# A hybrid convolution and retention layer on eight cores: weight sums on one engine, two products joined in PSUM, interleaved norm chains

## The reference

```
hcat = x @ w_in                                   # B, C, h | q, k, v, g, 512 columns each
y_conv = B * causal_conv3(C * h)
o = chunkwise retention of rotary(q), rotary(k), v (4 heads, chunks of 128)
y_ret = silu(g) * head_group_norm(o)
x = layer_norm(ALPHA * x + concat(y_conv, y_ret) @ w_out)
ff = square(relu(x @ w_ff1)) @ w_ff2              # 1024 -> 4096 -> 1024
ple = sigmoid(x @ w_ple_gate) * (p @ w_ple_proj)
x = layer_norm(ALPHA * x + ff + ple)
```

## Time and profile before

| | us |
|---|---|
| median of 6 runs | 880.86 |
| lowest, highest | 879.99, 882.60 |
| the profiled execution's own time | 880.31 |
| its span on the slowest core (core 4) | 878.8 |
| PE busy in it | 777.3 (88%) |
| DVE, POOL, ACT busy | 565.4, 299.5, 267.5 |

### The profile page before, as it was taken

The page is one execution under the profiler, slowest core; times in us unless marked ns, Lnnn a source line. Parts: engine busy times, 40 slices in busy tenths (PEclk is TensorE's granted clock), DMA queues, the critical chain, the costliest instruction groups (busy, mean ns, idle before and its releaser), DMA issues.

```text
span 878.8 us, 12280 instructions; the slowest of 8 cores (875.8 to 878.8 us)
## 1 busy us (share of the span) xinstructions
PE 777.3 (88%) x3884; PEld 363.4 (41%) x3960; DVE 565.4 (64%) x767; ACT 267.5 (30%) x499; POOL 299.5 (34%) x252
## 2 busy tenths in 40 slices
PE   4999999998998869878999999769999999999920
PEld 1444455554454324323444444324444444444400
DVE  4556745566655725555478999715764477999991
ACT  2222246646662154335332000113343322000021
POOL 9000046555653613341000125403661000124574
PEclk9999999999999989999999999899999999999965
DMA  9995215310029664546821540586679920441012
GB/s 125 162 194 104 59 38 89 57 46 28 26 74 256 103 131 99 141 121 132 144 49 28 94 83 13 106 158 120 178 170 229 164 51 12 85 75 22 1 72 119
DMA packets 22814, 86.97 MB, mean 99 GB/s; under 512 B 2784, under 2 KB 4960, under 8 KB 17376
## 3 DMA queue, kind: packets, MB, share of 16 engines
q0 software_dynamic: 13392, 60.82, 39.1%
q1 hardware_dynamic: 9216, 25.11, 8.7%
q10 hardware_dynamic: 144, 0.26, 0.1%
HBM read 123.93 MB, written 14.68 MB: 158 GB/s over the span
## 4 chain that ended last, share of the span: by engine, by line
PE 58%; DVE 15%; issue 8%; DMA 7%; POOL 6%; ACT 4%; DVEq 0%; SPq 0%; ACTq 0%; POOLq 0%
PE ps L178 56%; DVE ycat L185 4%; DMA x1b_53<-s_x 3%; DVE xacc L185 3%; DMA xT_56<-xT 2%; POOL xtmp L185 2%; PE ps L182 2%; DVE xacc L196 2%; DMA xin_118<-x 1%; POOL lnst L185 1%; DVE lnst L681 1%; DVE ring_106 L185 1%; ACT xtmp L207 1%; POOL xacc L185 1%; DVE lnst L1029 1%
## 5 line engine op out<-in xcount | busy, mean ns | idle before, releaser
L185 DVE TENSOR_TENSOR xacc<-xacc,ps 128x512 f32<-128x512 f32 x96 | 62.0, 680 | 32.1 <-PE ps L178 30.5
L207 ACT ACTIVATE xacc<-xacc,lnst 128x1024 f32<-128x1024 f32 x23 | 26.4, 1148 | 172.9 <-POOL lnst L185 141.0
L185 DVE TENSOR_TENSOR ycat<-hT 128x2048 bf16<-128x2048 bf16 x40 | 71.3, 1782 | 2.5
L178 PE MATMUL ps<-ring_104,ycat 128*128 128x512 bf16 x280 | 65.8, 379 | 4.0 <-DVE xtmp L196 1.9
L185 POOL TENSOR_TENSOR lnst<-lnst,neghalf 128x1 f32<-128x1 f32 x32 | 36.4, 1138 | 71.8 <-DVE lnst L189 71.7
L185 DVE TENSOR_TENSOR hT<-ps,tR_129 128x512 bf16<-128x512 f32 x43 | 29.6, 687 | 40.9 <-ACT tR_129 L207 40.9
L178 PE MATMUL ps<-ycat,ring_107 128*128 128x512 bf16 x251 | 55.6, 379 | 0.3
L185 DVE TENSOR_TENSOR hT<-ps,tR_128 128x512 bf16<-128x512 f32 x42 | 28.8, 686 | 39.8 <-ACT tR_128 L207 39.7
L185 DVE TENSOR_TENSOR hT<-ps,tR_127 128x512 bf16<-128x512 f32 x43 | 29.5, 686 | 36.2 <-ACT tR_127 L207 36.1
L207 ACT ACTIVATE ycat<-ps 128x1024 bf16<-128x1024 bf16 x16 | 16.4, 1024 | 112.5 <-PE ps L182 112.5
L178 PE MATMUL ps<-ycat,ring_106 128*128 128x512 bf16 x188 | 45.2, 397 | 1.6 <-ACT ycat L207 1.4
(11 more groups left out here) (287 smaller groups left out, 1567.0 us busy)
## 6 DMA issues: line engine op xcount, KB each, us to landing
ring_107<-w_ff POOLq DMA_DIRECT2D x6, 1024.0 KB, 11.0
ring_106<-w_ff POOLq DMA_DIRECT2D x5, 1024.0 KB, 10.6
ring_105<-w_ff POOLq DMA_DIRECT2D x5, 1024.0 KB, 11.2
xtmp<-x SPq DMA_DIRECT2D x8, 512.0 KB, 8.4
ring_108<-w_ff POOLq DMA_DIRECT2D x4, 1024.0 KB, 14.3
ring_109<-w_ff POOLq DMA_DIRECT2D x4, 1024.0 KB, 13.1
ring_104<-w_ff POOLq DMA_DIRECT2D x4, 1024.0 KB, 12.8
s_x1f<-xtmp SPq DMA_DIRECT2D x8, 512.0 KB, 7.5
```

Of the source, the lines that this page charges most:

```text
L178: self.P.op("pe", lambda e: e.matmul(out, lhsT=lhsT, rhs=rhs, start=start, stop=stop, skip_group_check=skip), reads, writes)
L185: self.P.op(eng, lambda e: e.tensor_tensor(out=out, in0=in0, in1=in1, op=op), reads, writes)
L207: self.P.op("act", lambda e: e.activation(out=out, in_=in_, func=func, **kw), reads, writes)
```

## The change

- `Queue` gets a number of lanes: `step` goes round the first `lanes` generators instead of finishing one after the other. Lanes are 2 in the mix stretch, 3 in `phase_ff1` of the first pass, 2 in that of the second, 1 in `phase_ff2` up to M4 and 2 in M7.
- All `wsum` calls run on DVE. M3 is only added to one block of the output and M6 is then summed onto M3's banks; M4 and M7 likewise. The order of products becomes M1 M5 M3 M6 M2 M4 M7, and banks are fixed: 4 to 7 for M5 and M2, 0 to 3 for the others.
- bf16 x1 of blocks 8 to 11 stays in four new `x2b` buffers (the bytes of `ln2w` and `ln2b`, which are loaded later); blocks 12 and 13 are loaded at the start of M3, 14 and 15 during M4.
- Eight instead of four `xin` buffers, the new four in the bytes of ring 2; the first slab of `w_ff1` is therefore loaded after the loop over `t`.
- Blocks 0 to 3 do the last two pieces of their first norm as one DVE instruction instead of ACT and POOL.
- `gen_out` is one generator per block, and its DMAs go from POOL's queue to SP's.

```
 class Queue:
+        self.lanes = 1
     def step(self, k=1):
+                self.n = (self.n + 1) % min(self.lanes, len(self.gens))
-                    next(self.gens[0])
+                    next(self.gens[self.n])
...
-    M3=(((0, 0),), (((0, 1), 1), ((1, 1), 1))),
-    M2=(((0, 1), (1, 1), 1), (((1, 0), 1), ((1, 1), -1))),
-    M6=(((0, 1), (0, 0), -1), (((1, 1), 1),)),
-    M4=(((1, 1),), (((0, 0), 1), ((1, 0), 1))),
-    M7=(((1, 0), (1, 1), -1), (((0, 0), 1),)),
+    M3=(((0, 0),), (((0, 1), 1),), False),
+    M6=(((0, 1), (0, 0), -1), (((1, 1), 1),), True),
+    M2=(((0, 1), (1, 1), 1), (((1, 0), 1), ((1, 1), -1)), False),
+    M4=(((1, 1),), (((1, 0), 1),), False),
+    M7=(((1, 0), (1, 1), -1), (((0, 0), 1),), True),
...
         def gen_ln(buf, rbuf, w_t, b_t, rw, rb, slot, spread=True):
             h.stt(buf, buf, mv[:, 0:1], w_t[:], ALU.subtract, ALU.mult, [rbuf, rl, rw], [rbuf])
             yield
+            if not spread:
+                h.stt(buf, buf, rstd, b_t[:], ALU.mult, ALU.add, [rbuf, rr, rb], [rbuf])
+                yield
+                return
...
             if b < 8:
-                load_xin(k + 4)
+                load_xin(k + 8)
...
+        def gen_norm1(b):
+            yield from gen_ln1(b)
+            if b < 12:
+                h.cp("act", x2b[b - 8][:], x1v(b), [x1r(b)], [("x2b", b - 8)])
+            else:
                 x1_cast(b)
...
             def before(m, i):
-                if at_ == ("M5", 0):
-                    bg.add(hsum("M2"))
-                if at_ == ("M5", 4):
+                if at_ == ("M5", 2):
                     bg.add(wsum(s_, 0, "S", "12", "22", ALU.subtract))
                     bg.add(wsum(s_, 1, "S", "12", "22", ALU.subtract))
                 if at_ == ("M3", 0):
+                    bg.add(wsum(s_, 0, "12", "12", "11", ALU.add))
+                    bg.add(wsum(s_, 1, "12", "12", "11", ALU.add))
                     bg.add(hsum("M6"))
-                    pool(wsum(s_, 0, "12", "12", "11", ALU.add, "pool"))
...
+                if at_ == ("M6", 0):
+                    load_slab("ff2", 3, wslot(s_, 1, "S")[0])
+                    bg.add(hsum("M2"))
                 if at_ == ("M2", 0):
-                    load_slab("ff2", 3, wslot(s_, 1, "S")[0])
-                    bg.add(wsum(s_, 1, "12", "12", "11", ALU.add))
-                if at_ == ("M6", 0):
-                    bg.add(wsum(s_, 0, "11", "S", "11", ALU.subtract))
-                    bg.add(wsum(s_, 1, "11", "S", "11", ALU.subtract))
+                    bg.add(wsum(s_, 0, "12", "S", "11", ALU.subtract))
+                    bg.add(wsum(s_, 1, "12", "S", "11", ALU.subtract))
                     bg.add(hsum("M7"))
-                if at_ == ("M6", 4):
-                    pool(wsum(s_, 0, "S", "S", "22", ALU.add, "pool"))
-                if at_ == ("M6", 6):
-                    pool(wsum(s_, 1, "S", "S", "22", ALU.add, "pool"))
+                    bg.add(wsum(s_, 0, "S", "S", "22", ALU.add))
+                if at_ == ("M4", 0):
+                    bg.add(wsum(s_, 1, "S", "S", "22", ALU.add))
+                    bg.step(2)
...
+                if at_ == ("M3", 0):
+                    load_x2b(12)
+                    load_x2b(13)
+                if m in ("M4", "M7") and i % 2 == 0:
                     n = (0, 4)[m == "M7"] + i // 2
-                    x1_transpose(8 + n, n, bank8(), "x2b")
-                    if n < 6:
-                        load_x1b(10 + n)
+                    b = (12, 13, 8, 9, 10, 11, 14, 15)[n]
+                    x1_transpose(b, b - 8, 4 + n % 4, True)
+                    if n < 2:
+                        load_x2b(14 + n)
...
+                b0 = 4 if m in ("M5", "M2") else 0
+                onto = PRODS[m][2]
-                        h.mm(ps[bank][:], lt, ring[si][:, k, :], c == 0, c == 15, rl + [rs],
-                             [RP[bank]])
-                    bg.step(2)
+                        h.mm(ps[bank][:], lt, ring[si][:, k, :], c == 0 and not onto, c == 15,
+                             rl + [rs], [RP[bank]], skip=onto)
+                    bg.step(3 if last and m in ("M4", "M7") else 2)
```

More of the change, by code:

```diff
@@ L379, in build_nc @@
            at("ln2w", [128, D], F32, o_rt, "ln2w"), at("ln2b", [128, D], F32, o_rt + 4 * KB, "ln2b")]
-    xin = [at("xin%d" % i, [128, 512], F32, o_cb + 8 * KB + i * 2 * KB, ("xin", i)) for i in range(4)]
+    xin = [at("xin%d" % i, [128, 512], F32, (o_cb + 8 * KB, o_wc + 16 * KB)[i // 4] + i % 4 * 2 * KB,
+              ("xin", i)) for i in range(8)]
+    x2b = [at("x2b%d" % i, [128, D], BF16, o_rt + i * 2 * KB, ("x2b", i)) for i in range(4)] + x1b
     xacc = at("xacc", [128, 8, D], F32, o_xT, [("xa", b) for b in range(8)])
@@ L814, in build_nc @@
                           ("lnt", i), [], [("ln1w", "ln1b")[i]])
-                wo = [use_slab("wout", g, 3) for g in range(2)]
-                for k in range(4):
+                wo = [use_slab("wout", g, 2) for g in range(2)]
+                for k in range(8):
                     load_xin(k)
@@ L833, in build_nc @@
                 mix_part(b, hf, wo[hf][0], wo[hf][1], next_bank())
[L834 to L839, removed]
+                bg.step(2)
+        for b in range(8, 16):
+            bg.add(gen_norm1(b))
         def phase_ff1(s_):
@@ L945, in phase_ff2 @@
             slab_n["use"] += 4
[L946 to L950, removed]
+            WB = dict(M1="S", M5="22", M3="S", M6="12", M2="11", M4="12", M7="S")
+            bg.lanes = 1
             def before(m, i):
@@ L981, in before @@
+                if last:
+                    return
+                if at_ == ("M4", 1):
                     prefetch(18)
-                if at_ == ("M7", 0) and not last:
+                if at_ == ("M7", 0):
                     prefetch(20)
-                if m in ("M4", "M7") and i % 2 == 0 and not last:
+                if at_ == ("M3", 0):
+                    load_x2b(12)
+                    load_x2b(13)
+                if m in ("M4", "M7") and i % 2 == 0:
                     n = (0, 4)[m == "M7"] + i // 2
-                    x1_transpose(8 + n, n, bank8(), "x2b")
-                    if n < 6:
-                        load_x1b(10 + n)
@@ L989, in before @@
[L989 to L993, removed]
+                    b = (12, 13, 8, 9, 10, 11, 14, 15)[n]
+                    x1_transpose(b, b - 8, 4 + n % 4, True)
+                    if n < 2:
+                        load_x2b(14 + n)
+                    if n == 5:
+                        for k in range(2):
+                            h.dma("sp", lnt[2 + k][:], (ln2_w, ln2_b)[k].partition_broadcast(128),
+                                  ("lnt", 2 + k), [], [("ln2w", "ln2b")[k]])
@@ L994, in phase_ff2 @@
+            for n, m in enumerate(PRODS):
                 jp = [(j, p) for j in range(2) for p in range(4)]
@@ L996, in phase_ff2 @@
                     jp = [(j, p) for p in range(4) for j in range(2)]
-                banks = {}
+                b0 = 4 if m in ("M5", "M2") else 0
+                onto = PRODS[m][2]
                 for i, (j, p) in enumerate(jp):
                     before(m, i)
-                    if p not in banks:
-                        banks[p] = bank8()
                     si, rs = wslot(s_, j, WB[m])
-                    bank = banks[p]
+                    bank = b0 + p
                     for k in range(8):
@@ L1014, in phase_ff2 @@
                             last_stats(p, 1)
-                        if last and m == "M6":
+                        if last and m == "M2":
                             last_stats(4 + p, 1)
@@ L1072, in build_nc, with gen_out @@
         outs = []
[L1074 to L1077, removed]
-                    h.dma("pool", out[b * 128:(b + 1) * 128, :], xacc[:, b, :], ("outq", b),
-                          [("xa", b)], [("out", b)])
-                    outs.append(("out", b))
-                if b >= 2:
-                    k = b - 2
-                    h.dma("pool", xacc[:, k, :], s_x1f[k // 4, (k % 4) * 128:(k % 4 + 1) * 128, :],
-                          ("xl", k), [("s_x1f", 8 + k)], [("xa", k)])
+        def gen_out(b):
+            yield from gen_ln(xacc[:, b, :], ("xa", b), lnt[2], lnt[3], "ln2w", "ln2b", b)
+            h.dma("sp", out[b * 128:(b + 1) * 128, :], xacc[:, b, :], ("outq", b),
+                  [("xa", b)], [("out", b)])
+            outs.append(("out", b))
+            for _ in range(2):
                 yield
+            h.dma("sp", xacc[:, b, :], s_x1f[b // 4, (b % 4) * 128:(b % 4 + 1) * 128, :],
+                  ("xl", b), [("s_x1f", 8 + b)], [("xa", b)])
+            yield
         for s_ in range(2):
@@ L1095, in build_nc @@
             if s_ == 0:
-                bg.add(gen_out())
+                for b in range(8):
+                    bg.add(gen_out(b))
         P.join("sp", outs)
```

74 lines of the change are left out of this document (40 added, 34 removed).

## The result

The changed kernel takes 839.84 us (median of 10 runs, 839.27 to 840.92) against 881.19 for the kernel before in the same runs: ratio 0.953, interval 0.9522 to 0.9539. The forecast was 838, and the range of 827 to 851 holds it.

What follows compares the result with a forecast made beforehand. PE bounds the kernel, busy over 99% in the two long stages, so gains come only where it idles: 2.5 + 5 + 7 + 17 + 11 = 42.5 off 880.3 us gives 837.8, forecast 838, range 827 to 851 (about 8 in 10).

Steps and rivals of the forecast that it cites:

- Loop: Loop, blocks 0 to 3: one DVE piece ends the first norm, PE's waits for `yn` go; gain 2.5 us, bounds 0 and 4.
- Mix stretch: 250 to 306.27 us: the 12.39 us `xin` load goes, DVE at most one group behind; gain 5 us, bounds 3 and 6.
- ff1: ff1 of the first pass: three norm chains share a lap of eight groups; gain 7 us, bounds 0 and 11.
- The wait for block 12's store: ff1 of the first pass: block 14's cast must wait for this store from the same buffer; gain cut from 8 to 7.
- M4 and M7: M4 and M7 of the first pass: 32.4 us instead of 49.78; gain taken as 17 us, bounds 10 and 18.
- the wait for bank 4: Start of M4, first pass: the first transpose waits until DVE empties this bank; 1.3 us lost.
- ff2 at 0: ff2, both passes: DVE's extra 2.9 us and M6's and M7's wait for banks cost PE 0 us.
- End: After the second pass's matmuls: first power 9.7 us earlier, seven blocks in 35.6; gain 11 us, bounds 8 and 17.
- POOL still the last to be waited for: Sign that the forecast is right: this holds in the last stage after the matmuls, which takes 25 to 31 us.
- A: Rival, ff1 laps: DVE pieces wait whole POOL adds, the gain of 7 becomes a loss of 5; 850 us, chance 0.15.
- B: Rival, M4 and M7: bank 4, late loads or sums of slot S keep half of 17 us; 846 us, chance 0.12.
- C: Rival, ff2: sums slow for another reason than POOL, DVE becomes the bound, kernel slower, up to 1020 us; chance 0.03.

## Why the prediction was right, step by step

- **Loop: failed.** 2.5 was taken, 0.37 came: the loop ends at 272.62 for 272.99. The step named the risk itself ("the DVE piece puts the masked scores 1.27 later, and PE meets them about 0.35 on") and priced it too low; PE waited 0.7 to 1.0 each time, which is nearly what its waits for `yn` had been.
- **Mix stretch: the size right (5.65 for 5), the reason in part wrong.** The 12.39 us load was read off the chain of waits as the first thing to remove. Four buffers bring a load of 11.28 back and nothing is lost. Which of the other parts brought the gain stays open.
- **ff1: right at 7.2 for 7**, and one lane at two pieces costs 7.7. That the difference came out this well is partly luck. The prediction took 15 lost before and 7 or 8 after; behind the stop at the start PE is idle 11.0 before and 3.8 after (the rows below, width less PE's busy time), so both terms were too large. The stall is elsewhere than told, too: the first two laps hide in the eight banks, and the third, of two chains, costs 1.40 and 2.35, then some 1.7 at the low clock (0.63 in 368.36 to 373). The wait for block 12's store, priced at 1, did not show.

```profile
324.50:402.66 78.16, 67.16 (x283) 27.89 (x290) 38.45 (x65) 31.74 (x47) 29.32 (x19) 0.96 0.46 113
...
318.25:389.47 71.22, 67.46 (x291) 29.37 (x292) 37.55 (x62) 36.46 (x52) 24.36 (x17) 0.94 0.58 133
```

- **M4 and M7: right, 32.37 for 32.4**, and the wait for bank 4 was 1.17 for 1.3. Four sums on DVE take 5.21 together, 1.30 each as told (1.22 is the time of one by itself). Both parts are needed, which the prediction had not split.
- **ff2 at 0: right within 0.5.** M6 met its banks in time. The 0.98 that PE lost is in M7, where the last norms held DVE. Nothing was gained by joining products either.
- **End: right at 10.5 for 11.** The first power comes 793.73 - 711.65 = 82.1 after M1's start (81.2 told), 8.8 earlier than before. From M1's start to the end 10.05 are won (126.45 for 136.50), so this is the whole gain but 1.3. The seven blocks take 36.7 (35.6 told, 37.1 before): they are not quieter. "POOL still the last to be waited for" was half of it; DVE and POOL wait for each other.
- **Rivals.** A's mechanism was real but sat at the end, where it was there before too (a DVE piece of 2.82 and POOL adds of up to 3.38), not in the laps of ff1, where DVE's pieces read 1.28. B and C did not come.

So the total is off by 1.8 us of 42.5: 2.1 too much in the loop, and misses of up to 0.7 elsewhere that nearly cancel. It was right because the large terms were widths of stalls read stage by stage against what the matmuls alone take.

## What to carry to other kernels

Price a stall by comparing a stage's width with its matmuls alone, then ask for each part of a change what stands next in line; a load on the chain can be worth nothing once removed. Where DVE instructions with two SBUF inputs and POOL work meet, put DVE's one-input work beside POOL's by the order of emission, before moving work between engines. Spread a background chain so that its return time fits the work it hides behind: lanes and pieces per group are one choice.

## What the hardware showed unexpectedly

- A POOL power on one element per partition, 0.55 alone, takes 1.45 to 1.52 when a DVE instruction with two SBUF inputs is in flight, and ends some 0.4 after it (805.68 after 805.28 in the changed kernel).
- Two streams of large sums on DVE and POOL alternate whole instructions: 4.9 to 5.1 us each on either engine for what takes DVE 1.22 alone.
- After these stops PE runs on at 1.2 GHz: granted clock 0.50 from 318.25 to 324 behind the five stops at ff1's start, 0.50 from 547 to 553 behind the 13.5 us stop, so each of the two costs some 3 us more than its waits. Without the stops the clock reads 1.00. The price varies: behind the same five stops the run with the other order of the last norms is back at 1.00 by 321.2. Nor does every row of stops bring it: in the kernel before, ten waits for `hT` of up to 1.8 us left the clock at 1.00 (a stretch of that kernel, then one of the run).

```profile
382.00:392.00 10.00, 7.31 (x31) 2.72 (x30) 5.07 (x10) 4.04 (x6) 3.81 (x2) 1.00 0.93 203
...
321.20:324.00 2.80, 2.80 (x15) 1.26 (x14) 0.69 (x1) 2.37 (x3) 0.59 (x1) 1.00 0.00 0
```
